# A decoder layer with a routed mixture of experts: one 1 MB load of expert weights moved from ahead of five stores to behind the loads that follow the first gathers

## The reference, cut to what matters

```python
y = hres + hier_moe(rms_norm(hres, p['norm2']), ...)

def hier_moe(x, rg_w, rg_b, re_w, re_b, w1, w3, w2):
    # 4 groups of 4 experts: the best group of a row, and in it the two best experts
    pg = softmax(t @ rg_w + rg_b);  g_oh = one_hot(top_k(pg, 1))
    le_sel = einsum('ng,nge->ne', g_oh, t @ re_w + re_b)
    e_val, e_idx = top_k(le_sel, 2);  wts = softmax(e_val) * pg_top
    h = silu(einsum('nd,edf->nef', t, w1)) * einsum('nd,edf->nef', t, w3)
    return einsum('nef,efd->nd', h * gate[..., None], w2)
```

## Time and profile before

| | us |
|---|---|
| runs, median of 3 | 791.31 (790.29 to 791.31) |
| the profiled execution, its own time | 790.43 |
| its span, first to last instruction | 788.5 |
| PE busy in the span | 762.8 |
| DVE, POOL, ACT busy | 382.4, 294.9, 225.5 |
| mean granted TensorE clock | 0.990 of full speed |

### The profile page before, as it was taken

One profiled execution on the slowest core, in us unless ns is written; L12 is line 12 of the kernel. 1 busy time (PEld: TensorE's weight loads), 2 busy tenths in 40 slices (PEclk: granted clock), 3 DMA queues, 4 the chain that ended last, 5 costly groups with the idle time before them and its releaser, 6 DMA issues.

```text
span 788.5 us, 14312 instructions
## 1 busy us (share of the span) xinstructions
PE 762.8 (97%) x5277; PEld 545.0 (69%) x5277; DVE 382.4 (48%) x713; ACT 225.5 (29%) x436; POOL 294.9 (37%) x221
## 2 busy tenths in 40 slices
PE   8999999999999999999999999999999799999992
PEld 7887778676677888777767788888888634333330
DVE  4637777677497689543534113734533712031210
ACT  4131344342423454142414223322201512020100
POOL 0000331364553975255524554434250112332314
PEclk9999999999999999999999999999999999999996
DMA  9342662355665542245535453342761899999933
GB/s 363 119 162 82 204 195 86 85 159 168 184 178 188 169 137 66 80 150 175 174 122 174 122 190 141 100 159 69 267 267 51 310 337 410 371 389 370 384 116 50
DMA packets 72538, 148.32 MB, mean 188 GB/s; under 512 B 13335, under 2 KB 47144, under 8 KB 70420
## 3 DMA queue, kind: packets, MB, share of 16 engines
q1 hardware_dynamic: 65716, 135.43, 49.9%
q0 software_dynamic: 5920, 10.82, 5.6%
q10 hardware_dynamic: 832, 1.16, 0.5%
HBM read 137.71 MB, written 18.90 MB: 199 GB/s over the span
## 4 chain that ended last, share of the span: by engine, by line
PE 92%; DMA 3%; ACT 2%; DVE 1%; issue 1%; POOL 0%; SPq 0%; POOLq 0%; ACTq 0%
PE ps L874 23%; PE ps L608 17%; PE ps L1215 11%; PE ps L843 7%; PE ps L1120 6%; PE ps L1285 5%; PE ps L651 3%; PE ps L623 3%; PE ps L900 2%; PE ps L597 2%; PE ps L678 1%; PE ps L1204 1%; DMA scr_x<-cst 1%; PE ps L707 1%; PE ps L694 1%; DMA tmp<-in_xT 1%
## 5 line engine op out<-in xcount | busy, mean ns | idle before, releaser
L608 PE MATMUL ps<-xn,ring 128*128 128x268 f32 (+1 forms) x576 | 136.5, 391 | 0.2 <-ACT qk L1378 0.2
L608 PEld LDWEIGHTS ps<-xn,ring 128*128 128x128 f32 x576 | 106.9, 190 | 24.5 <-issue 4.2
L2576 POOL TENSOR_TENSOR kv<-kv,sgd 128x1024 f32<-128x1024 f32 (+1 forms) x32 | 80.4, 2526 | 98.8 <-DVE tmp L1848 51.7
L1530 ACT ACTIVATE sgt<-sgt,vec 128x260 f32<-128x260 f32 x60 | 30.1, 510 | 122.8 <-DVE sgt L2129 70.8
L2691 POOL DMA_INDIRECT out_y<-cst,gtab x24 | 37.3, 1555 | 70.9 <-DVE cst L2498 42.0
L843 PE MATMUL ps<-br,ring 128*128 128x260 f32 x256 | 61.0, 386 | 0.6 <-DVE sgt L2133 0.6
L874 PE MATMUL ps<-xn,ring 128*128 128x260 f32 x240 | 58.0, 385 | 0.0
L874 PE MATMUL ps<-xn,qb 128*128 128x260 f32 x240 | 57.6, 383 | 0.1
L843 PEld LDWEIGHTS ps<-br,ring 128*128 128x128 f32 x256 | 47.8, 190 | 11.2 <-issue 3.2
L1876 DVE TENSOR_REDUCE sgd<-kv 128x32 f32<-128x1024 f32 (+1 forms) x32 | 40.7, 1279 | 21.4 <-POOL kv L2576 21.4
L874 PEld LDWEIGHTS ps<-xn,qb 128*128 128x128 f32 x240 | 45.4, 190 | 7.4 <-issue 0.4
(11 more groups left out here) (525 smaller groups left out, 1499.6 us busy)
## 6 DMA issues: line engine op xcount, KB each, us to landing
ring<-in_w_mg SPq DMA_DIRECT2D x32, 640.0 KB, 4.7
kv<-in_kc SPq DMA_DIRECT2D x128, 128.0 KB, 2.3
kv<-in_vc SPq DMA_DIRECT2D x128, 128.0 KB, 2.1
ring<-in_w_in SPq DMA_DIRECT2D x24, 512.0 KB, 5.0
kv<-in_w SPq DMA_DIRECT2D x8, 1024.0 KB, 13.1
br<-in_w SPq DMA_DIRECT2D x7, 1024.0 KB, 12.9
sgd<-in_w SPq DMA_DIRECT2D x6, 1024.0 KB, 14.4
qk<-in_w SPq DMA_DIRECT2D x6, 1024.0 KB, 11.0
```

Of the source, the lines that this page charges most:

```text
L608: mm = pe.matmul(ps[:, 2 * (t % 2) + h, 0:hw], wsl(c, k), xnv[:, k, col0 + h * hw:col0 + (h + 1) * hw], start=(k == 0), stop=(k == KT - 1))
L1530: act.activation(g, g, ACT.Sigmoid, bias=vv(V_BM + 8 * "ABCD".index(n) + m + i)).then_inc(g_a, 1)
L2576: pool.tensor_tensor(kb, kb, qbc[:, b:b + 1, :].to_broadcast([P, HALF // 2 + (half and u), 256]), ALU.mult)\
```

## The change

Load 14 with its wait for `outs` is moved: from between load 9 and the five stores to `scr_x`, to behind load 13 and in front of load 15. Nothing else is touched; `STREAM` stays 15.

```diff
@@ -536,8 +536,6 @@
             sp.wait_ge(op_mm, len(OUT_ORDER) * KT // 2)
             weights(8)
             weights(9)
-            sp.wait_ge(outs, 16 * POOL_OUTS)
-            weights(STREAM - 1)
             for b in range(NB):
                 sp.wait_ge(tt_a, b + 1)
                 sp.dma_start(scr_x[b * RB:(b + 1) * RB, :], tk[b]).then_inc(xs_ok, 16)
@@ -553,6 +551,8 @@
             sp.wait_ge(y_out, 16 * NB)
             weights(12)
             weights(13)
+            sp.wait_ge(outs, 16 * POOL_OUTS)
+            weights(STREAM - 1)
             for n in range(STREAM, 12 * QUADS):
                 weights_used(n - STREAM)
                 weights(n)
```

## The result

The changed kernel takes 794.89 us (median of 22 runs, 789.99 to 798.12), the kernel before 791.44 (22 runs, 789.51 to 793.64). The ratio is 1.0041 with a 95% interval of 1.0030 to 1.0052: slower by 3.4 us, where 2.7 us less was forecast. Three of its 22 runs (790.0, 790.8 and 791.9 us) are about as quick as the kernel before. The profiled execution took 794.89 us, its span is 793.0.

The account below looks back on a forecast made before the run. PE was taken to set the time almost everywhere, with the DMA queue full during the experts; 1.2 us from an earlier start and 1.5 us from the clock took 791.31 to 788.6 us, range 787.6 to 791.4.

Parts of the forecast that it names:

- The stores: Ahead of the first gather: with 1.05 MB less queued, the last store to `scr_x` lands 3.06 us sooner, near 622.9 us.
- The table: `from_row`, which DVE writes until 625.27 us for the first gather; it lets only 0.70 us of 3.06 through.
- The start of the products: Transposes ahead of the first expert products: they begin 1.2 us sooner, between 0.70 and 1.29.
- the lower bound: First gather's landing unchanged at 4.75 us, so the transposes gain only 0.70 us.
- The clock: First 32 expert products: the fall to half clock at 632.6 us doesn't come, 1.5 us gained, between 0 and 1.7.
- The added load: Full queue from 640 us: load 14 costs 2.6 to 2.9 us, loads behind it net about 1.5 us later.
- The rival's price of 5.8 us: Last loads late: load 14's 2 KB rows cost twice a whole load's time, load 47 at 764.6 us; chance 0.11.
- the sooner start: Loads 10 to 13, waiting for gather 2 and the last residual store, should come 0.7 to 2 us sooner.
- The end: Quad 3's last products: load 47 lands at 760.3 us, wanted at 760.7, so PE waits for no weights.
- Slack: Before the change, load 47 lands at about 758.8 us and its readers begin at 763.40: 4.6 us.
- the two shifts: At load 47: landing about 1.5 us later, and its readers in PE 2.7 us sooner.
- the clock's 1.7 us: Last 96 products, if PE idles ahead of them for late loads: possible further loss to a fallen clock, 1.7 us.

## Why the prediction was wrong, step by step

**The stores: right.** The last increment of `xs_ok` came 16.3 and 15.3 us after load 8's issue, and 18.8 and 18.4 before: 2.1 to 3.5 us sooner, 3.06 was the forecast. The table (L2444) was late next, as said: it starts 17.9 us after load 8's issue in the changed kernel's first trace and in both of the kernel before, and the gather went at 19.05 against 19.65 and 19.29 before.

**The start of the products: the mechanism right, the size not.** The gather still took 4.64 us, so the lower bound held and not the upper, which I took: the transposes began 23.8 us after load 8's issue against 24.5 and 24.4, 0.6 us sooner and not 1.2. That is in an execution where the table is as early as before. In the second trace of the changed kernel the clock is at half during the router's work,

```profile
622.40:629.20 6.80, 6.08 (x37) 5.25 (x38) 3.90 (x19) 1.02 (x1) 1.64 (x2) 0.50 0.41 144
```

the table comes at 19.2 us and the transposes begin at 25.3, later than in either trace of before, in spite of the sooner stores. A gain that ends at the table is one only as far as the table is on time.

**The clock: wrong as a gain of the change.** The first 32 products did take 3.64 us. But that was luck: they took 3.64 us also in the two kernels that repeat a load, with the stores in their old place, and 4.87 in the changed kernel without load 47. In the profiled execution of the change the clock had fallen earlier instead, from 619.9 to 623.3 us and from 626.7 to 630.1, where PE transposes rows:

```profile
619.90:623.30 3.40, 3.40 (x18) 3.35 (x17) 2.96 (x13) 2.17 (x4) 0.55 (x1) 0.50 0.82 289
626.70:630.10 3.40, 3.40 (x18) 3.02 (x19) 2.99 (x18) 1.02 (x1) 2.09 (x2) 0.50 0.51 147
```

In every trace it falls once, twice or three times between 618 and 636 us, at places that move with the execution; I read one fall in one trace as the price of one idle stretch. In both stretches PE is busy without a gap, and all but two of its products are transposes of `rows_of`; but that is in part what the half clock does, since the 24 that begin at 619.1 us take 4.47 us, and 2.81 us at the full clock in the kernel before. What came ahead of both falls were mostly short products of the router with gaps between them: PE is busy for 2.82 us from 616.5 to 619.9 us, and for 2.17 from 623.3 to 626.7. The Trainium skill, "TensorE: Matmul & The Clock Gate", Part 4, by which transposes do not count for the clock as matmuls do, is the rule that I weighed against my 1.5 us, and set aside. Falls among transposes go with it; that the kernel before ran the same transposes at clock 1.00 speaks against it as the whole reason. No run changed the transposes, so what makes the clock fall here stays open.

**The added load: this is the step that failed.** "Net the loads behind 14 are about 1.5 us later, between 0.6 and 2.9": load 47 landed 5.8 to 8.2 us later (157.3 and 158.8 against 151.6 and 150.6), above the upper bound. The rival's price of 5.8 us, which I gave 0.11, is what the first pair of traces has, but not for its reason, which was that rows of 2 KB cost twice the time: a whole load in 8 KB rows made load 47 5.2 us late. Two errors in it. I priced the load by the rate of the full queue, 2.6 to 2.9 us, and that is right for the next load behind it in the first traces: load 15 landed 2.8 us later (50.5 against 47.7 us; 4.4 in the second traces, where the gathers were late). But a load has landed when its slowest share has, and during the row adds the shares drift apart: load 30 landed from 88.9 to 96.4 us before and from 90.8 to 105.5 with the change; without the adds, from 86.8 to 90.1 and from 88.1 to 92.1. The other error is the sooner start that I set against it. In the profiled execution load 10 did land sooner, 34.9 against 36.4 us, but load 13 landed at 45.2 us in both: the lead was gone before load 14 was paid. Besides, 2 to 3 us of lateness are there in the kernel without load 14 too (153.4 us), which the prediction has in no term and no run explains.

SP's list of waits from 640 us on shows the same from the other side. For PE to free a buffer it waited, with the change:

```profile
SPq L510 <- PE ps L1215: 23.5, 8, 4.8
SPq L510 <- PE ps L1285: 16.2, 2, 12.5
```

and in the kernel before:

```profile
SPq L510 <- PE ps L1215: 29.8, 9, 8.7
SPq L510 <- PE ps L1285: 29.4, 3, 13.3
SPq L513 <- PE ps L1215: 4.3, 1, 4.3
```

63.5 us of waiting have become 39.7 (63.2 and 45.1 in the second traces). SP stands longer at its issues: loads 45 and 46 take it 5.25 us, and 2.15 before. In the kernel before it then still waited 4.2 us for PE to free load 47's buffer; with the change it is behind PE there, waits for nothing and issues load 47 at 136.5 us after load 8 and not at 134.3.

**The end.** Slack was 4.6 us, as read. PE arrived 2.1 us sooner in the profiled execution (0.5 in the second), the load landed 5.8 later, so PE waited 3.7 us; and the half clock behind the wait took 1.76 us more of the last 96 products. PE starts them 1.6 us later than before (157.7 against 156.1) and ends them 3.3 us later, of which 3.0 are left at the end: the stage from load 8's issue to the end is 184.3 us against 181.3, and 186.1 against 182.0 in the second traces. "Load 47 just in time, so I cost it at nothing" was the sentence to distrust: with the two shifts in it the margin was 0.4 us, between bounds 2.3 us apart, and the loss on the far side had the clock's 1.7 us on top, while the near side had nothing to win.

The Trainium skill's rule on issuing early ("DMA: Bandwidth & Descriptors", Rules for kernel authors) speaks for the old place, and the runs agree: ahead of the stores load 14 cost 0.2 to 0.6 us of the gather's issue, since of the 2.1 to 3.5 us by which it delayed the stores the rest went into the wait for the table.

**What stays open.** Which of the DMA engines fall behind during the row adds, and why, no run told; nor how much of the difference between load 14's copy and load 9's (158.2 and 156.3 us) is the size of its rows; nor why load 47 is 2 to 3 us later without any added load once the stores come sooner. That the price of load 14 grows from 2.8 us to 5.8 and more over the stage because of the adds rests on the two traces without them, one of each kernel, in which it is 1.6 us at load 15 and at load 46; why it swings in between with them is open too.

## What to carry to other kernels

A transfer that is early is hardly in the way if what it delays isn't wanted yet: before moving it back, read when the thing behind it was wanted anyway (here the table let 0.2 to 0.6 us of the 3 through to the gather), and whether the queue runs empty soon after. A load added to a stage whose queue is full can delay the last of that stage by more than its bytes (here 2.6 us by bytes over rate, and 5.8 to 8.2 measured beside the row adds); where two arrivals are forecast within a microsecond of each other, price the miss as well as the hit. Where a forecast rests on a clock fall at one place, look at a second trace of the same kernel first.

## What the runs showed that I had not expected

The same instructions up to load 8 take 606.9 to 610.5 us, and one of the differences is a fall of the clock at about 255 us that some executions have and some have not, at 10.00 of 10 us of PE work. Without the row adds load 46 lands at 133.7 us instead of 147.2, 13.5 us sooner. Up to these landings POOL's queue moved 4.3 MB without the adds and 7.3 MB with them; 3 MB at 401 GB/s would be an estimated 7.5 us. So the adds hold up the weights by nearly twice what their bytes would say. (Load 47's 4.6 us from issue to landing, instead of 17.3, says less: without the adds all the loads ahead of it had landed when it was issued.) And where the time seemed to be had most cheaply, between the stores and the gather, the same 1 MB cost 2.66 us of a gather's landing.
